# Expert weight pieces laid out as four consecutive rows to a partition, with permuted transposes

## The chip, the core and the metric

The kernel runs on one core of one Trainium2 chip. The metric is the device time of one execution in microseconds (us), as a median over runs. TensorE is PE in the rows, its weight loads are PEld, VectorE is DVE, ScalarE is ACT, GpSimd is POOL, and SyncE, which issues most DMAs here, is SP.

## What is computed

Two sequences of 512 tokens with 1024 features go through a trunk of two layers, all in fp32. Each layer has an attention mixer (latent and window attention in the first, dilated and neighbourhood attention in the second) and then a mixture of 16 experts, in which each expert chooses its 64 best tokens of a sequence:

```
aff = softmax(xt @ w_router);  gate, idx = top_k(aff.T, 64)
xe = xt[idx]
g = xe @ w_gate[e];  u = xe @ w_up[e]              # 1024 x 1024 each
ye = (silu(g) * u) @ w_down[e] * gate
y = zeros.at[idx].add(ye)
```

The two sequences share the weights, so the kernel handles one expert with 128 rows: 64 of the one sequence and 64 of the other.

## The kernel before

The program is a row of stages with a barrier on all engines between them: project, two attention kinds, output (with the router), choose (top 64), experts; then the same for the second layer, and a last norm. The change touches only the two `experts` stages and the helper `load_piece` (L1392), which the stages before them call too, for the first pieces.

An expert has three weight matrices of 1024 x 1024 fp32 (4 MB each). Each is cut by rows into halves of 512 rows, so there are six pieces of 2 MB: gate lo and hi, up lo and hi, down lo and hi. SBUF has a ring with one place for each piece, 16 KB to a partition. A piece is stored as `p c n`: partition p holds four weight rows of 1024 elements, c = 0 to 3. Before the change, slot (p, c) of a piece holds row c * 128 + p of its half.

A product with a piece (`product`, L1475 to 1482) runs c = 0 to 3 and, for each c, two matmuls of 512 columns. The stationary operand is column block `lhs[:, 4 * half + c, :]` of the turned input (128 contraction rows by 128 tokens), the moving operand half a weight row of each partition. The contraction runs over the partitions, so row p of the turned block has to be the feature whose weights lie at (p, c).

The turned inputs are made by `turn` (L1465 to 1470): eight PE transposes of 128x128 in two groups of four, for the gathered rows x of the next expert (into `xT`) and for the hidden rows h of the expert before (into `hT`). A transpose loads 128 columns of the input as stationary operand and streams the 128x128 identity through. ACT copies bank 0 to the first half of the turned tile, DVE bank 1 to the second.

The order of PE in one round e is written by hand: gate lo(e), turn h(e-1), gate hi(e), down lo(e-1), down hi(e-1), up lo(e), turn x(e+1), up hi(e). SP issues the load of a piece as soon as PE has finished with the piece in that place, and the new piece is used one round later. POOL gathers the 128 rows of the next expert from `normed` by an indirect DMA (L1591) and adds the results of the expert before to `residual` by another (L1609). In this trace one fp32 matmul of 512 columns appears as two LDWEIGHTS and two MATMUL records, and one fp32 transpose as one of each.

Of the kernel before, what the change touches and what calls it, by code (L numbers as in the profile page):

```python
# [30 lines left out]
P = 128  # L31
D = 1024
# [19 lines left out]
E = 16  # L52
CAP = 64
F = 1024
# [4 lines left out]
class Steps:  # L59
# [35 lines left out]
    def done(self, name, instruction):  # L95

        step = 1
        while self.names[self.told % self.per] != name:
            assert self.names[self.told % self.per] in self.left_out, name
            self.told += 1  # L100
            step += 1
        self.told += 1
        while self.told % self.per and self.names[self.told % self.per] in self.left_out:
            self.told += 1
            step += 1
        instruction.then_inc(self.sem, step)


def hybrid_trunk(nc, x_in, norm_mix, norm_ffn, norm_final, w_in_ab, q_norm, w_uq, kv_norm, w_ukv, sink,
                 w_out_ab, w_in_cd, rpb_padded, w_out_cd, w_router, w_gate, w_up, w_down,  # L110
                 rope_table, window_table, dilated_table, column_table, y_out):
    with ExitStack() as ctx:
        def sb(name, shape, dt=F32):
            return ctx.enter_context(nc.sbuf_tensor(name, shape, dt))
# [7 lines left out]
        def at(a, offset, pattern):  # L122
            return bass.AP(a.tensor, offset, pattern)
# [8 lines left out]
        ident = sb("ident", [P, P])  # L132
# [7 lines left out]
        bank = [ctx.enter_context(nc.psum_tensor(f"bank{b}", [P, BANK], F32)) for b in range(8)]  # L140
# [955 lines left out]
        def output(inputs):  # L1096
# [47 lines left out]
            def sp(eng):  # L1144
                tile = [[D, P], [1, D]]
                inputs.load_rows(eng, 1)

                load_piece(eng, inputs.layer, 0, 0)
                load_piece(eng, inputs.layer, 0, 1)

                def store_x(t, s):
# [18 lines left out]
                store_x(T - 1, 1)  # L1170
                store_h(T - 1, 1)
                load_piece(eng, inputs.layer, 0, 2)
                load_piece(eng, inputs.layer, 0, 3)
                for s in range(2):
# [217 lines left out]
        def load_piece(eng, layer, e, k):  # L1392
            w, half = SOURCES[k]
            eng.dma_start(ring[:, k * PIECE:(k + 1) * PIECE].rearrange("p (c n) -> p c n", c=4),
                          at(w, (e + layer * E) * (D * F) + half * (D * F // 2), [[F, P], [P * F, 4], [1, F]])
                          ).then_inc(piece_in[k], 16)

        def experts(layer, follow=None):
# [65 lines left out]
                        follow(eng, k)  # L1464

            def turn(eng, src, k, done):
                for c in range(4):
                    mm = eng.transpose(bank[k][:, c * P:(c + 1) * P],  # L1468
                                       src[:, (4 * k + c) * P:(4 * k + c + 1) * P], ident[:, :])
                done(mm)  # L1470

            def pe(eng):
                def body(e, j, left_out):
# [15 lines left out]
                    if "h0" not in left_out:  # L1489
                        for k in range(2):  # L1490
                            eng.wait_ge(dve_s.sem, dve_s.after(f"hidden{k}", e - 1))
                            turn(eng, hidden, k, lambda mm: pe_s.done(f"h{k}", mm))
# [7 lines left out]
                    if "up lo" not in left_out:  # L1500
                        product(4, xT[j], 2, 0, "up lo", e)
                        eng.wait_ge(rows_in[1 - j], e * 8 + (24 if j else 16))
                        for k in range(2):
                            turn(eng, rows[1 - j], k, lambda mm: pe_s.done(f"x{k}", mm))
                        product(4, xT[j], 3, 1, "up hi", e)

                eng.wait_ge(rows_in[0], 16)
                turn(eng, rows[0], 0, lambda mm: mm.then_inc(pe_s.sem, 1))
                turn(eng, rows[0], 1, lambda mm: mm.then_inc(pe_s.sem, 2))
                rounds(eng, pe_s, body)  # L1510
# [292 lines left out]
```

## Time and profile before

| | us |
|---|---|
| median of 3 runs | 2979.7 |
| lowest and highest run | 2979.1, 2984.41 |
| span of the profiled execution | 2978.9 |
| PE busy in the profiled execution | 2808.6 (94%) |
| PE busy in the matmuls of the expert products, L1479 | 1334.7 |
| weight pieces loaded | 192 of 2048 KB |

The profile is of one execution. A row of it sums instructions that have one line and one operation; a stretch (from : to, in us from the start of the span) gives the busy time of each engine in it. The middle of the first expert stage is 742 to 1380 us, and of the second 2260 to 2905 us. "issue" in the rows is waiting that the profile puts down to nothing it shows.

### The profile page before, as it was taken

What the parts mean: (1) busy time and instruction counts of PE and PEld (TensorE: products, weight loads), DVE (VectorE), ACT (ScalarE), POOL (GpSimd) and SP (SyncE); (2) the same over time, 40 slices, a digit from 0 to 9 for tenths busy, and PEclk for the clock granted to TensorE, in tenths of its full rate; (3) what the DMA queues carried; (4) which work ended last, traced back from release to release, by engine and by line L of the source; (5) the groups of instructions that cost most, each with busy time, mean ns of one, the idle gap of its engine ahead of it and who ended that gap; (6) DMA issues with size and microseconds to landing.
All of it is one profiled execution on the core that took longest, in us unless ns stands there. A gap on an engine that the chain in (4) does not pass through costs nothing. (4 is left out here: it accounts for less than half of the span.)

```text
span 2978.9 us, 31400 instructions
## 1 busy us (share of the span) xinstructions
PE 2808.6 (94%) x9840; PEld 1528.3 (51%) x9840; DVE 968.4 (33%) x2002; ACT 497.4 (17%) x1147; POOL 245.4 (8%) x457
## 2 busy tenths in 40 slices
PE   8998999996999999997999989999978999999994
PEld 5665777553444444443444447676543444444442
DVE  2223567224332233222111115554233233323322
ACT  1212446110000000000011014443110000000001
POOL 2221000000000000000000000010000000000002
PEclk9999999997999999998999999999988999999997
DMA  5324243436889988996221132223346998998875
GB/s 182 93 72 115 77 127 102 160 115 254 312 315 323 316 315 315 320 319 238 77 84 45 41 126 57 82 81 128 115 181 228 316 323 311 318 324 314 315 264 190
DMA packets 243226, 594.91 MB, mean 200 GB/s; under 512 B 28640, under 2 KB 101600, under 8 KB 243168
## 3 DMA queue, kind: packets, MB, share of 16 engines
q1 hardware_dynamic: 233664, 559.56, 53.1%
q0 software_dynamic: 9504, 34.61, 4.9%
q8 instruction: 33, 0.54, 0.1%
q14 instruction: 25, 0.20, 0.0%
HBM read 520.72 MB, written 77.07 MB: 201 GB/s over the span
## 5 line engine op out<-in xcount | busy, mean ns | idle before, releaser
L1479 PE MATMUL bank<-ring,arena 128*128 128x512 f32 x3072 | 1334.7, 594 | 3.7 <-issue 1.9
L1479 PEld LDWEIGHTS bank<-ring,arena 128*128 128x128 f32 x3072 | 580.4, 191 | 711.2 <-issue 709.0
L517 PE MATMUL bank<-ring,arena 128*128 128x512 f32 (+3 forms) x1440 | 554.5, 544 | 1.8 <-DVE arena L674 0.9
L517 PEld LDWEIGHTS bank<-ring,arena 128*128 128x128 f32 x1440 | 272.7, 192 | 259.0 <-issue 221.2
L1199 PE MATMUL bank<-ring,arena 128*128 128x512 f32 x512 | 229.7, 603 | 2.2 <-DVE arena L1274 2.2
L1554 DVE RECIPROCAL arena<-arena 128x512 f32<-128x512 f32 x64 | 214.6, 3353 | 2.2
L960 PE MATMUL bank<-arena 128*128 128x512 f32 (+2 forms) x384 | 187.2, 581 | 13.9 <-SPq L187 10.8
L1542 DVE COPY arena<-bank 128x512 f32<-128x512 f32 x66 | 45.6, 691 | 415.8 <-PE bank L1468 415.8
L973 PE MATMUL bank<-arena 128*128 128x64 f32 x1344 | 173.9, 269 | 1.2
L967 PEld LDWEIGHTS bank<-ident,arena 128*128 128x128 f32 x928 | 115.3, 143 | 114.6 <-issue 83.8
L973 PEld LDWEIGHTS bank<-arena 128*128 128x128 f32 x1344 | 165.1, 192 | 6.5 <-DVE arena L1041 4.9
L992 ACT ACTIVATE arena<-arena 128x512 f32<-128x512 f32 (+1 forms) x192 | 127.6, 664 | 190.2 <-DVE arena L1041 111.8
L1514 ACT ACTIVATE arena<-bank 128x512 f32<-128x512 f32 x66 | 39.4, 597 | 701.9 <-PE bank L1468 701.9
L1199 PEld LDWEIGHTS bank<-ring,arena 128*128 128x128 f32 x512 | 96.5, 193 | 113.3 <-issue 113.3
L967 PE MATMUL bank<-ident,arena 128*128 128x128 f32 x928 | 145.8, 276 | 5.0 <-ACT arena L992 3.6
L1021 DVE CUSTOM_DVE_ANT_0 arena<-bank,arena 128x512 f32<-128x512 f32 (+1 forms) x192 | 118.9, 620 | 54.8 <-PE bank L960 39.3
L616 ACT ACTIVATE arena<-bank 128x512 f32<-128x512 f32 (+2 forms) x104 | 57.8, 571 | 468.5 <-PE bank L517 275.1
L1609 POOL DMA_INDIRECT residual<-arena x32 | 51.0, 1594 | 1025.8 <-DVE arena L1560 1025.8
L674 DVE COPY arena<-bank 128x512 f32<-128x512 f32 (+3 forms) x72 | 42.8, 609 | 221.4 <-PE bank L517 155.9
L1031 DVE COPY arena<-bank 128x512 f32<-128x512 f32 (+2 forms) x128 | 82.0, 640 | 91.9 <-PE bank L967 91.1
L1552 DVE TENSOR_SCALAR arena<-arena 128x512 f32<-128x512 f32 x64 | 27.0, 422 | 241.1 <-ACT arena L1524 241.1
L1568 DVE TENSOR_TENSOR arena<-bank,arena 128x512 f32<-128x512 f32 x64 | 41.2, 686 | 196.5 <-PE bank L1479 196.5
(114 smaller groups left out, 1659.8 us busy)
## 6 DMA issues: line engine op xcount, KB each, us to landing
ring<-in_w_gate SPq DMA_DIRECT2D x64, 2048.0 KB, 8.3
ring<-in_w_up SPq DMA_DIRECT2D x64, 2048.0 KB, 9.2
ring<-in_w_down SPq DMA_DIRECT2D x64, 2048.0 KB, 10.3
ring<-in_w_in_cd SPq DMA_DIRECT2D x6, 2048.0 KB, 17.7
arena<-residual SPq DMA_DIRECT2D x24, 512.0 KB, 5.6
arena<-in_x_in SPq DMA_DIRECT2D x16, 512.0 KB, 5.7
mixed<-arena SPq DMA_DIRECT2D x32, 256.0 KB, 2.4
arena<-mixed SPq DMA_DIRECT2D x16, 512.0 KB, 4.2
```

The source lines that it names most:

```text
L517: mm = eng.matmul(bank[bank_of[name]][:, 0:width], lhs(c), rhs_of(c), start=(c == 0), stop=(c == chunks - 1))
L616: act_s.done(name, eng.activation(out, bank[bank_of[name]][0:rows, 0:width], ACT.Copy, **scale))
L960: pe_s.done(f"qk{u}", eng.matmul(bank[u % 4][:, 0:(b1 - b0) * P].rearrange("p (b n) -> p b n", n=P), q[s][:, t, e, :], k[s][:, b0:b1, 0 if ...
L967: mm = eng.transpose(bank[4 + u % 2][:, b * P:(b + 1) * P], p[u % 4][:, b, :], ident[:, :])
L973: mm = eng.matmul(bank[6 + u % 2][:, 0:HD], pT[u % 2][:, b, :], v[s][:, b0 + b, e * HD:(e + 1) * HD], start=(b == 0), stop=(b == b1 - b0 - 1))
L992: act_s.done(f"exp{u}", eng.activation(flat(p[u % 4], n), src, ACT.Exp, bias=stat[:, 0, u:u + 1], scale=-1.0 if biased else 1.0, accum_out ...
L1021: dve_s.done(f"max{u}", eng.tensor_tensor_reduce(flat(masked[u % 4], n), bank[u % 4][:, 0:n], bias, -1.0, BIG, ALU.add, ALU.min, stat[:, 0 ...
L1031: dve_s.done(f"turn{u}", eng.tensor_copy(flat(pT[u % 2], n), bank[4 + u % 2][:, 0:n]))
L1199: mm = eng.matmul(bank[2 + k][:, :], oT[s][:, c, :], wo_ring[:, c, k * BANK:(k + 1) * BANK], start=(c == 0), stop=(c == DC - 1))
L1479: mm = eng.matmul(bank[first_bank + b][:, :], lhs[:, 4 * half + c, :], piece[k][:, c, b * BANK:(b + 1) * BANK], start=(half == 0 and c == ...
L1554: dve_s.done(f"sig{k}", eng.reciprocal(sig[:, half], sig[:, half]))
L1609: eng.indirect_dma_start(out=residual, out_offset=bass.IndirectOffsetOnAxis(ap=index[1 - j], axis=0), in_=y[1 - j], in_offset=None, comput ...
```

## The change

`load_piece` now takes its source with a partition step of four rows: slot (p, c) of a piece holds row 4 * p + c of its half, so the four rows of a partition are one run of 16 KB in HBM, in place of four runs of 4 KB that lie 512 KB apart. The bytes, the places in SBUF, the semaphores and the number of DMAs are the same. To match, the transposes take as stationary operand every fourth column: column p of block (k, c) is feature 512 * k + 4 * p + c, where it was 512 * k + 128 * c + p. In SBUF the 128 elements of one partition that a transpose reads are then 16 bytes apart, where they were 4 bytes apart. The turned tiles keep their shape, and the products, the copies on ACT and DVE and the gathers and scatters are unchanged. `load_piece` is used for all six pieces, and `turn` for x and for h, so both inner dimensions are permuted in the same way as their weights; the output columns of the matrices are not permuted.

```diff
             eng.dma_start(ring[:, k * PIECE:(k + 1) * PIECE].rearrange("p (c n) -> p c n", c=4),
-                          at(w, (e + layer * E) * (D * F) + half * (D * F // 2), [[F, P], [P * F, 4], [1, F]])
+                          at(w, (e + layer * E) * (D * F) + half * (D * F // 2), [[4 * F, P], [F, 4], [1, F]])
                           ).then_inc(piece_in[k], 16)
...
             def turn(eng, src, k, done):
+                columns = src.rearrange("t (h p c) -> t h c p", h=2, c=4)
                 for c in range(4):
-                    mm = eng.transpose(bank[k][:, c * P:(c + 1) * P],
-                                       src[:, (4 * k + c) * P:(4 * k + c + 1) * P], ident[:, :])
+                    mm = eng.transpose(bank[k][:, c * P:(c + 1) * P], columns[:, k, c, :], ident[:, :])
                 done(mm)
```

No instruction moves on any engine. On SP, at the end of the first output stage and the start of the first expert stage, the pieces' DMAs stand where they stood:

```order
-L1394 DMA ring<-in_w_up 128x4x1024 x2
-L1394 DMA ring<-in_w_down 128x4x1024 [waits abo_x_out1,abo_x_out0,stage_ended]
-L1394 DMA ring<-in_w_down 128x4x1024
-L1394 DMA ring<-in_w_gate 128x4x1024 [waits pe_steps,stage_ended]
-L1394 DMA ring<-in_w_gate 128x4x1024 [waits pe_steps]
-L1394 DMA ring<-in_w_up 128x4x1024 [waits pe_steps] x2
+L1394 DMA ring<-in_w_up 128x4096 x2
+L1394 DMA ring<-in_w_down 128x4096 [waits abo_x_out1,abo_x_out0,stage_ended]
+L1394 DMA ring<-in_w_down 128x4096
+L1394 DMA ring<-in_w_gate 128x4096 [waits pe_steps,stage_ended]
+L1394 DMA ring<-in_w_gate 128x4096 [waits pe_steps]
+L1394 DMA ring<-in_w_up 128x4096 [waits pe_steps] x2
```

Only the shape differs: four runs of 1024 elements to a partition have become one of 4096. The waits and their order are the same. On PE the rows are the same but for the line number of the transpose.

## Rows read from the trace of the kernel before

**Rows 1.** Busy time by stretch: first stage start, both expert middles.

```profile
core 0: us, PE busy (x) PEld busy (x) DVE busy (x) ACT busy (x) POOL busy (x), PEclk, DMA share, GB/s
660.00:700.00 40.00, 10.02 (x52) 9.03 (x51) 21.63 (x56) 2.91 (x8) 4.19 (x12) 0.56 0.71 262
...
742.00:1390.00 648.00, 646.14 (x1684) 298.92 (x1683) 184.05 (x165) 44.53 (x75) 45.02 (x73) 1.00 0.89 312
...
2260.00:2905.00 645.00, 645.00 (x1683) 298.76 (x1682) 190.67 (x169) 44.93 (x76) 43.04 (x70) 1.00 0.88 309
```

**Rows 2.** PE in order of time, 959 to 990 us: start, length, line, count.

```profile
959.45 22.48 PE L1479 MATMUL bank<-ring,arena 128*128 128x512 f32 x52
981.76 1.04 PE L1468 MATMUL bank<-ident,arena 128*128 128x128 f32 x8
982.63 7.89 PE L1479 MATMUL bank<-ring,arena 128*128 128x512 f32 x18
```

**Rows 3.** The page's costliest group: busy, mean ns of one, idle before.

```profile
L1479 PE MATMUL bank<-ring,arena 128*128 128x512 f32 x3072 | 1334.7, 594 | 3.7 <-issue 1.9
```

**Rows 4.** What SP and PE waited for, whole span: total us, times, longest.

```profile
SPq L1394 <- PE bank L1479: 1190.1, 178, 20.9
...
PE bank L1468 <- DMA arena<-normed,arena: 12.4, 2, 6.3
```

**Rows 5.** Transposes of the experts by line: ns min/median/max, first and last start.

```profile
L1468 PEld LDWEIGHTS bank<-ident,arena x528: 138/140/230, 698.3 to 2926.8; 128*128 128x128 f32 x176
L1468 PE MATMUL bank<-ident,arena x528: 272/273/448, 698.4 to 2926.9; 128*128 128x128 f32 x176
```

**Rows 6.** Weight loads of other lines: 48 columns, and 128 for a matmul.

```profile
L1222 PEld LDWEIGHTS bank<-ident,arena x8: 103/103/113, 584.3 to 2220.1; 128*48 128x48 f32 x8
L973 PEld LDWEIGHTS bank<-arena x1344: 186/192/192, 422.3 to 2067.2; 128*128 128x128 f32 x192
```

**Rows 7.** Weight loads in a row, in order of time: moving 64 and 16 wide.

```profile
431.19 0.75 PEld L973 LDWEIGHTS bank<-arena 128*128 128x128 f32 x6
659.78 1.75 PEld L1229 LDWEIGHTS bank<-arena 128*128 128x128 f32 x15 [0.24 <-issue]
```

**Rows 8.** SP in order of time, 958 to 1026 us: pieces issued.

```profile
961.49 0.37 SPq L1394 DMA_DIRECT2D ring<-in_w_gate  x1
...
1004.44 0.37 SPq L1394 DMA_DIRECT2D ring<-in_w_gate  x1
```

**Rows 9.** Landing times of a piece (L1394), whole span.

```profile
DMA to landing us min/median/max: 7.7/9.2/17.4
```

**Rows 10.** DMA queues, 742 to 1380 us: packets, MB, share of 16 engines.

```profile
DMA packets 51039, 198.30 MB, mean 311 GB/s; under 512 B 1856, under 2 KB 1856, under 8 KB 51037
...
q1 hardware_dynamic: 46861, 183.06, 78.3%
q0 software_dynamic: 4176, 15.21, 10.1%
```

**Rows 11.** POOL in order of time, 958 to 1050 us: scatter, index, gather.

```profile
976.79 1.59 POOL L1609 DMA_INDIRECT residual<-arena  x1 [31.02 <-DVE arena L1560]
986.11 0.19 POOL L1600 COPY arena<-chosen 128x1 uint32 x1 [7.72 <-DMA residual<-arena]
...
987.50 0.99 POOL L1591 DMA_INDIRECT arena<-normed,arena  x1 [0.81 <-POOL arena L1583]
1019.74 1.60 POOL L1609 DMA_INDIRECT residual<-arena  x1 [31.25 <-DVE arena L1560]
```

**Rows 12.** PE's next turn of x, in order of time.

```profile
1024.71 1.04 PE L1468 MATMUL bank<-ident,arena 128*128 128x128 f32 x8
```

**Rows 13.** Landing times of the gather (L1591), whole span.

```profile
DMA to landing us min/median/max: 4.4/5.5/8.3
```

**Rows 14.** Start of the first expert stage: the last early pieces, the first gather.

```profile
672.93 0.92 SPq L1394 DMA_DIRECT2D ring<-in_w_down  x2
...
693.81 1.22 POOL L1591 DMA_INDIRECT arena<-normed,arena  x1 [0.99 <-POOL arena L1583]
```

## The prediction, made before the changed kernel was run

> **What bounds the kernel now.** I first took the busy time by stretch, to see who is full where the change acts. In the middle of both expert stages PE is busy for 646.14 of 648 us and for all of 645 us, at full granted clock, while the DMA engines are busy for 0.89 and 0.88 of the time [rows 1]. Both are high, so it has to be read which one waits for the other. The list of waits says it: SP, about to load a piece, waited 1190.1 us in total for PE to free the place [rows 4], and PE's only wait for a DMA in these stages is 12.4 us, twice at a stage's start, for the first gathered rows. So the weight stream follows PE, and PE is the bound.
>
> The order of time on PE then gives the price of its two kinds of work. 52 records of a product take 22.48 us; with the length of the last one, 0.59 us [rows 3], taken off, the step is (22.48 - 0.59) / 51 = 0.429 us. Eight transposes take from 981.76 to 982.63, 0.87 us, or 0.109 us each, with no gap on either side [rows 2]. A round of one expert is 96 records of products (48 matmuls of two) and 16 transposes: 96 x 0.429 + 16 x 0.109 = 42.9 us, and two scatters in a row start 42.95 us apart [rows 11]. The round has nothing in it but PE's own stream.
>
> **The load, part one of the change.** It touches 192 pieces of 2 MB. In the middle of the first stage the queue of these loads moved 183.06 MB in 46861 packets, 3.9 KB on the mean [rows 10], that is the runs of 4 KB. Runs of 16 KB can make packets longer and the transfer shorter, but who would use the time? A gate piece is issued at 961.49, when its place is free, and the same place is issued again at 1004.44 [rows 8]. The piece is first needed 16 records (6.9 us) before that, at about 997.5, so 36 us after it was issued; it lands after 9.2 us in the median and 17.4 at most [rows 9]. A faster landing takes time from a slack of 19 us or more, and the load that follows waits for PE all the same. So I cost the load at nothing, from both sides: the gain is nothing since no PE wait ends with a piece, the loss is nothing as long as the stream keeps up. The cover for that is the DMA time that is idle: the two queues use 78.3 + 10.1 = 88.4%, so the loads may use 11.6/78.3 = 15% more engine time [rows 10]. Nothing at the ends is saved either. The first gather starts at 693.81, the last early pieces were issued by 673.85 [rows 14], so even a landing of 17.4 us is over before it.
>
> **The transposes, part two.** This part lies on PE's own stream, so here each nanosecond counts: 528 transposes [rows 5] in 66 bursts of eight. The identity that streams through is read as before. What becomes strided is the stationary operand, the weight load, with 128 elements 16 bytes apart. No row shows a strided load, so I bound it.
>
> Is the load what sets the step of 109 ns? The load's record is 140 ns in a transpose [rows 5], 192 ns in a matmul and 103 ns for 48 columns [rows 6]. A fixed part is hidden in these. In stretches where the moving side is short, loads of the matmul kind stand in a row: (0.75 - 0.19) / 5 = 0.112 us apart with 64 moving columns and (1.75 - 0.19) / 14 = 0.111 us with 16 [rows 7]. So such a load occupies the path for 112 ns and overlaps the matmul before it completely; the step is the longer of load and stream, not their sum. A transpose's load has a record about 50 ns shorter. It thus occupies about 112 - 52 = 60 ns; by columns, (140 - 103) / 80 x 128 = 59 ns. I take half a matmul's load, 56 ns, and keep 60 as the other end. Under a step of 109 ns the load has about 50 ns to spare. The first load of each burst also lies under a matmul step of 429 ns, so at most 7 steps of a burst can grow: 7 x 66 = 462 steps.
>
> The ends are: no effect, 0 us; twice as long, max(109, 112) = 112 ns, 462 x 3 ns = 1.4 us (at 60 ns: 120 - 109 = 11 ns, 5.1 us); four times as long, as if the skipped elements were read too, 224 ns, 462 x 115 ns = 53 us (at 60 ns: 131 ns, 61 us). A gain is excluded, since the identity's stream stays. I take the doubled load, 1.4 us: it is the nearest to rows that exist, the loads of 112 ns [rows 7].
>
> The Trainium skill speaks on this very stride, in the page "SBUF — State Buffer", section "Door 1: The DMA port swizzle": SBUF lines are 16 bytes, an access that goes to a new line pays a penalty, at least two accesses to a line are needed to hide the latency, and yet a step of 4 fp32 is named as free. The change puts each fp32 into a line of its own, just at that step. By the first half of the rule the load grows, as in my first rival; by the second the cost is 0 and the time 2979.7. No row of this trace has such a read, so it can't say which half holds for weight loads.
>
> The results of a transpose are the same in shape, so the copies on ACT and DVE keep their length, and every wait behind them stands under a product of 6.9 us as before.
>
> **The sum.** Profiled span 2978.9 us, plus 0 for the loads, plus 1.4 for the transposes, makes 2980.3. The median of the runs shown is 0.8 us over that execution, which gives **2981.1 us**. A measurement of this kernel can tell some 0.2% (6 us) from no change, so this is "the same".
>
> **Rivals.**
>
> 1. *The strided weight load becomes the bound of the transposes* (slower). It decides from the point where a load takes more than 109 ns, some 1.9 times its length now. At three times, 168 ns, it costs 462 x 59 ns = 27 us, 3007 us; at four times 53 us, **3033 us**. For it: each read uses 4 of 16 consecutive bytes, and PE has no slack at all to hide it [rows 1]. Against it: the load uses only about half of the step. I split it: 15% that it lies between (2986 to 3025 us), 19% that it is about fourfold (3027 to 3042 us).
>
> 2. *The weight stream becomes slower than PE.* Runs of 16 KB change which parts of HBM the 16 DMA engines read side by side, and no row shows such a pattern. From 15% on more engine time the stream would be the bound. At 25% more, the loads take 42.9 x 0.783 x 1.25 = 42.0 us a round and the indirect DMAs 42.9 x 0.101 = 4.3, so 46.3 in place of 42.9: 3.4 x 32 = 109 us, 3090 us. Nothing speaks for it but that it isn't shown; longer runs rather cost less. 4%.
>
> 3. *The indirect DMAs come late.* If packets of 16 KB go ahead of each packet of a gather or scatter, these take longer. Their chain is: scatter at 976.79, over by 986.11, gather at 987.50 [rows 11], landed 5.5 us later [rows 13], its rows turned at 1024.71 at the earliest [rows 12]. It has 31.7 us to spare, twice what scatter and gather take now together, so they would have to become three times as long. I give it no more than 1% of the chance, within the 4% of rival 2.
>
> 4. *The packets don't become longer*, if a run is cut into 4 KB again. Then the load part does nothing at all, and the time is that of the transposes alone; it can't be told from the forecast by time, only by the number of packets.
>
> 5. *Faster.* The only PE wait with a DMA at its end is that of 6.3 us at each stage's start [rows 4]; a less loaded HBM may shorten it a little, and for more than 6 us it would have to vanish in half. I give 4% to this and to anything that I don't see: 2967 to 2973 us.
>
> **How the numbers follow.** Forecast, including rival 4: 58%, 2977 to 2986 us. Rival 1: 15% between and 19% at about 3033 us. Rivals 2 and 3: 4%. Faster: 4%. The forecast and the part between hold 73%, so the range must take in the fourfold load: 2976 to 3038 us; of the likeliest case alone it is 2977 to 2986 us. Within 0.2%: 58% and a small part of the case between, 60%. Slower: 13 + 19 + 4 = 36%. Faster: 4%.
>
> **What would show it.** In the profile of the changed kernel: the landing of a piece and its packets (128 packets of 16 KB to a piece, or 512 of 4 KB) show part one; SP's wait for PE stays near 1190 us or grows. The eight transposes of a burst take 0.87 to 0.90 us from start to next product if I am right, and 1.7 us in the fourfold case; the load's record grows from 140 ns by what the stride adds, and shows that even where the step hides it. Two scatters stay 42.95 us apart, against 44.6 us in the fourfold case. A PE wait that ends with a DMA of `ring` would prove rival 2, one with a gather in the middle of a stage rival 3.

## The result, and the profile after

| | before | changed |
|---|---|---|
| median, 9 runs each | 2980.81 us | 2988.38 us |
| lowest to highest | 2979.10 to 2984.41 | 2986.93 to 2991.72 |
| profiled span | 2978.9 | 2985.7 |
| ratio, with its 95% interval | | 1.0024 (1.0014 to 1.0033) |

The change makes the kernel slower by a quarter of a percent, 7.1 us by the ratio. It lies inside the range (2976 to 3038 us) but above what I held likeliest (2981.1 us; 2977 to 2986 us), and just over the 0.2% within which I had put "no change".

Long runs did come about. The page's section 2 and the landing times of a piece in the changed kernel:

```profile
DMA packets 169498, 594.91 MB, mean 199 GB/s; under 512 B 28640, under 2 KB 101600, under 8 KB 144864
...
DMA to landing us min/median/max: 7.3/8.6/16.5
```

The page before had 243226 packets. The 73728 that are gone are 384 for each of the 192 pieces: 128 packets of 16 KB in place of 512 of 4 KB. A piece lands after 8.6 us where it took 9.2 [rows 9]. The stretches that answer to [rows 1] show who gained by that:

```profile
core 0: us, PE busy (x) PEld busy (x) DVE busy (x) ACT busy (x) POOL busy (x), PEclk, DMA share, GB/s
742.00:1390.00 648.00, 646.14 (x1676) 301.95 (x1675) 184.11 (x165) 44.56 (x75) 45.10 (x73) 1.00 0.86 311
2260.00:2905.00 645.00, 645.00 (x1678) 301.75 (x1677) 185.93 (x166) 44.96 (x76) 43.15 (x70) 1.00 0.85 309
```

Nobody did. DMA's share fell from 0.89 and 0.88 to 0.86 and 0.85, PE is as full as before, and in the same 648 us it got through 1676 matmul records in place of 1684. SP's wait for PE grew from 1190.1 us [rows 4] to 1201.9:

```profile
SPq L1394 <- PE bank L1479: 1201.9, 178, 21.1
```

Most of the loss is in the transposes. First the order of time on PE, as in [rows 2], then the records of the transposes (L1469 is L1468 of before), as in [rows 5]:

```profile
981.53 1.11 PE L1469 MATMUL bank<-ident,arena 128*128 128x128 f32 x8
982.48 7.89 PE L1479 MATMUL bank<-ring,arena 128*128 128x512 f32 x18
```

```profile
L1469 PEld LDWEIGHTS bank<-ident,arena x528: 195/211/231, 697.0 to 2931.8; 128*128 128x128 f32 x176
L1469 PE MATMUL bank<-ident,arena x528: 272/284/461, 697.0 to 2931.9; 128*128 128x128 f32 x176
```

A burst of eight now takes 982.48 - 981.53 = 0.95 us to the next product, where it took 0.87. Over all 66 bursts the medians are 0.953 and 0.873 us, and 66 x 0.080 makes 5.3 us. The weight load's record went from 140 to 211 ns. Not all steps of a burst grew. These are the loads of one burst, first before and then changed:

```profile
981.33 0.14 PEld L1468 LDWEIGHTS bank<-ident,arena 128*128 128x128 f32 x1 [0.24 <-issue]
981.76 0.80 PEld L1468 LDWEIGHTS bank<-ident,arena 128*128 128x128 f32 x7 [0.28 <-issue]
```

```profile
981.10 0.20 PEld L1469 LDWEIGHTS bank<-ident,arena 128*128 128x128 f32 x1 [0.24 <-issue]
981.53 0.92 PEld L1469 LDWEIGHTS bank<-ident,arena 128*128 128x128 f32 x7 [0.23 <-issue]
```

The first load stands alone, under the last matmul of the product, and the other seven follow with the transposes. From the start of one transpose to the next, the medians over all bursts are 109 ns for the first step, as before, then 117, 122 and five times 121 ns. So seven steps grew, by 11.4 ns on the mean.

The rest of the span's 6.8 us shows at the very ends of the expert stages, where PE makes two short pauses before its last 32 records. In the changed kernel, first and second stage:

```profile
1378.47 1.26 PE L1469 MATMUL bank<-ident,arena 128*128 128x128 f32 x8 [0.96 <-DVE arena L1568]
1380.62 15.54 PE L1479 MATMUL bank<-ring,arena 128*128 128x512 f32 x32 [0.90 <-ACT arena L1514]
```

```profile
2930.93 1.26 PE L1469 MATMUL bank<-ident,arena 128*128 128x128 f32 x8 [0.96 <-DVE arena L1568]
2933.08 15.67 PE L1479 MATMUL bank<-ring,arena 128*128 128x512 f32 x32 [0.90 <-ACT arena L1514]
```

In the kernel before, the second of these places reads:

```profile
2925.99 1.16 PE L1468 MATMUL bank<-ident,arena 128*128 128x128 f32 x8 [0.96 <-DVE arena L1568]
2928.05 13.97 PE L1479 MATMUL bank<-ring,arena 128*128 128x512 f32 x32 [0.90 <-ACT arena L1514]
```

The same 32 records, with the same pauses ahead, take 15.54 and 15.67 us, not 13.97. It is the clock. Stretches of the changed kernel there (length, PE busy, PEclk, DMA share, GB/s):

```profile
2933.00:2936.00 3.00, 2.92 (x4) 0.58 0.00 0
2936.00:2939.00 3.00, 3.00 (x7) 0.86 0.00 0
```

The granted clock of 0.58 and 0.86 means that PE ran at 1.2 GHz for a part of these stretches and at 2.4 in the rest; before, it stood at 1.00 throughout. That is 1.6 + 1.7 = 3.3 us. Together with the 5.3 us it is more than the 6.8 us by which the spans differ; the stretches outside the experts came out 1.8 us shorter in this execution (the first turn starts at 697.00 in place of 698.36, and the way from the first expert stage to the second takes 0.4 us less).

### The profile page after: what moved, and what is told of

Same layout as the page of the kernel before. It is cut to its first block and busy times, and to the rows that moved or that the text cites. A ratio compares the mean times of both kernels' runs of the same rounds, so it can differ in the third digit from the quotient of the medians.

```text
span 2985.7 us, 31400 instructions
## 1 busy us (share of the span) xinstructions
PE 2815.2 (94%) x9840; PEld 1537.4 (51%) x9840; DVE 968.9 (32%) x2002; ACT 497.7 (17%) x1147; POOL 245.9 (8%) x457
```

## The experiments

My theory was that the strided weight load costs 5.3 us by itself and the long runs cost and give nothing. The rival was that part of the loss comes with the loads.

**One part alone: the long runs.**

```diff
-                          at(w, (e + layer * E) * (D * F) + half * (D * F // 2), [[F, P], [P * F, 4], [1, F]])
+                          at(w, (e + layer * E) * (D * F) + half * (D * F // 2), [[4 * F, P], [F, 4], [1, F]])
```

> Loads in runs of 16 KB, transposes of consecutive columns as before; the rows of the weights no longer match the columns, so the products are of mismatched rows. Theory (the whole loss lies in the strided weight load of the transposes): a burst of eight transposes takes 0.87 us as before, pieces take 128 packets and land in about 8.6 us, and the time is that of before, within 1 us. Rival (a part of the loss comes with the long runs, by their traffic beside PE or by the clock at the end of the expert stages): 1.5 to 3.5 us slower than before.

Measured: 2982.33 us beside 2981.05 for the kernel before, ratio 1.0002 (0.9993 to 1.0011). The load's record is 140 ns, and the burst takes 984.61 - 983.74 = 0.87 us:

```profile
983.74 1.04 PE L1468 MATMUL bank<-ident,arena 128*128 128x128 f32 x8
984.61 13.90 PE L1479 MATMUL bank<-ring,arena 128*128 128x512 f32 x32
```

Pieces landed in 8.6 us. Both stages ended with 13.97 us for the last 32 records. The long runs alone change nothing that can be told from the noise. The interval of the ratio reaches up to 3.3 us, so by the time alone a small loss isn't excluded; the records show none, neither in the bursts nor at the stage ends.

**The other part alone: the strided transposes**, with loads of 4 KB runs (the change to `turn` only).

> Loads in runs of 4 KB as before, transposes of every fourth column; rows and columns do not match here either. Theory: bursts of 0.95 us, the record of a transpose's load at 211 ns, and 5 to 7 us slower than before, the same as the changed kernel. If the last 32 product records of a stage take 15.6 us in place of 14.0 here too, the clock drop comes from the changed bursts and not from the loads. Rival (part of the loss is the long runs'): at most 5 us slower, and the stage ends as before.

Measured: 2988.01 us, ratio 1.0021 (1.0012 to 1.0030), about the whole loss of the change. Bursts take 0.95 us and the load's record is 211 ns. The first stage ended in 13.97 us, the second in 15.67:

```profile
2932.52 1.25 PE L1469 MATMUL bank<-ident,arena 128*128 128x128 f32 x8 [0.96 <-DVE arena L1568]
2934.68 15.67 PE L1479 MATMUL bank<-ring,arena 128*128 128x512 f32 x32 [0.90 <-ACT arena L1514]
```

So the loss comes with the strided transposes. The clock drop can come without the long runs, and it doesn't come each time.

**Another spacing: two rows together, columns 8 bytes apart.**

```diff
-            eng.dma_start(ring[:, k * PIECE:(k + 1) * PIECE].rearrange("p (c n) -> p c n", c=4),
-                          at(w, (e + layer * E) * (D * F) + half * (D * F // 2), [[4 * F, P], [F, 4], [1, F]])
+            eng.dma_start(ring[:, k * PIECE:(k + 1) * PIECE].rearrange("p (j c n) -> p j c n", j=2, c=2),
+                          at(w, (e + layer * E) * (D * F) + half * (D * F // 2), [[2 * F, P], [2 * P * F, 2], [F, 2], [1, F]])
...
-                columns = src.rearrange("t (h p c) -> t h c p", h=2, c=4)
+                columns = src.rearrange("t (h j p c) -> t h j c p", h=2, j=2, c=2)
...
-                    mm = eng.transpose(bank[k][:, c * P:(c + 1) * P], columns[:, k, c, :], ident[:, :])
+                    mm = eng.transpose(bank[k][:, c * P:(c + 1) * P], columns[:, k, c // 2, c % 2, :], ident[:, :])
```

> Two consecutive rows to a partition twice (runs of 8 KB), transposes of every second column, 8 bytes apart, matched. If the cost depends on how many 16-byte pieces are read, two columns share one, and the load stays hidden under the step of 109 ns: bursts of 0.87 us, the load's record between 140 and 175 ns, time as before within 1 us. Rival (any stride above one costs the same): record 211 ns, bursts 0.95 us, 5 us slower than before.

Measured: 2986.55 us, ratio 1.0018 (1.0009 to 1.0027). The records:

```profile
L1469 PEld LDWEIGHTS bank<-ident,arena x528: 194/209/231, 699.9 to 2935.2; 128*128 128x128 f32 x176
```

That is the rival's case: two columns in one 16-byte piece help next to nothing, the load takes 209 ns and a burst 0.94 us (the median of 66).

**A third spacing: every eighth column, 32 bytes apart.** The rows of a piece are 8 * p + 4 * half + c, so runs stay at 16 KB. A group of four transposes now reads from both halves of the hidden rows, so PE waits for both before the first group.

```diff
-                          at(w, (e + layer * E) * (D * F) + half * (D * F // 2), [[4 * F, P], [F, 4], [1, F]])
+                          at(w, (e + layer * E) * (D * F) + half * (4 * F), [[8 * F, P], [F, 4], [1, F]])
...
-                columns = src.rearrange("t (h p c) -> t h c p", h=2, c=4)
+                columns = src.rearrange("t (p c) -> t c p", c=8)
...
-                    mm = eng.transpose(bank[k][:, c * P:(c + 1) * P], columns[:, k, c, :], ident[:, :])
+                    mm = eng.transpose(bank[k][:, c * P:(c + 1) * P], columns[:, 4 * k + c, :], ident[:, :])
...
+                        eng.wait_ge(dve_s.sem, dve_s.after("hidden1", e - 1))
                         for k in range(2):
-                            eng.wait_ge(dve_s.sem, dve_s.after(f"hidden{k}", e - 1))
```

> Row 8 * p + 4 * half + c, runs of 16 KB at a pitch of 32 KB, transposes of every eighth column, 32 bytes apart, matched; the h turns wait for both halves of the hidden rows. If the load pays per 16-byte piece and every column already has one of its own at stride 4, nothing grows: record 211 ns, bursts 0.95 us, time as the changed kernel within 1.5 us. Rival (the cost grows with the distance): record of 320 ns or more, bursts over 1.5 us, 40 us slower or more.

Measured: 2981.15 us, ratio 1.0001 (0.9992 to 1.0010): as fast as the kernel before, and neither theory had that. Its records and a burst:

```profile
L1469 PEld LDWEIGHTS bank<-ident,arena x528: 185/188/226, 697.4 to 2926.9; 128*128 128x128 f32 x176
```

```profile
980.95 1.04 PE L1469 MATMUL bank<-ident,arena 128*128 128x128 f32 x8
981.83 13.90 PE L1479 MATMUL bank<-ring,arena 128*128 128x512 f32 x32
```

The load is longer than the 140 ns of neighbouring columns but shorter than the 211 ns of every fourth, and a burst takes 0.88 us. By the medians it is 8 ns longer than before (0.881 us), the last steps at 111 to 112 ns in place of 109, which makes 0.5 us in all. So the load's record grew by 48 ns and the steps hardly at all, as the prediction had it: a longer load costs nothing until it is longer than the identity's stream.

**Two odd spacings**, with the same loads and the transposes at `src[:, 4 * k + c : 4 * k + c + s * P]`, each s-th element, s = 3 and 7.

> As the kernel with columns eight apart (runs of 16 KB at 32 KB pitch), but the transposes read every third element, so they don't match the weights: only the spacing in SBUF is tried. Columns 2 and 4 apart cost a load record of 209 and 211 ns and bursts of 0.95 us, columns 8 apart 188 ns and bursts of 0.87 us. Theory A (any spacing but 1 takes twice the stream, and two or more reads in the same 32 bytes cost more on top): 12 bytes apart has nearly three reads in 32 bytes, so about 205 ns and 0.94 us. Theory B (the extra is of powers of two that meet a second reader at the same place): between 188 and 200 ns and bursts of 0.87 to 0.90 us.

> The same with every seventh element, 28 bytes apart: 1.14 reads in 32 bytes. Theory A: about 191 ns and bursts of 0.87 to 0.88 us, near the case of eight. Theory B gives the same or less. A record over 205 ns would speak against both and for a cost that the start address or the order of the reads sets.

Here too rows and columns do not match, and PE waits as with every eighth column. Measured: 2985.24 us for s = 3 and 2989.42 us for s = 7, one run each, beside 2982.52 for the kernel before. Single runs can't be compared closely, so the records have to decide:

```profile
L1468 PEld LDWEIGHTS bank<-ident,arena x528: 188/196/226, 699.6 to 2931.1; 128*128 128x128 f32 x176
```

```profile
L1468 PEld LDWEIGHTS bank<-ident,arena x528: 196/216/230, 696.5 to 2932.2; 128*128 128x128 f32 x176
```

The first is s = 3, with bursts of 0.90 us, the second s = 7, with bursts of 0.97 us. Theory A (reads in the same 32 bytes cost more) wanted about 205 and 191 ns, and theory B wanted both below 200; both fall with the 216 ns of s = 7. All spacings together:

| elements apart | load's record, median ns | burst of eight, median of 66, us |
|---|---|---|
| 1 | 140 | 0.873 |
| 2 | 209 | 0.944 |
| 3 | 196 | 0.904 |
| 4 | 211 | 0.953 |
| 7 | 216 | 0.969 |
| 8 | 188 | 0.881 |

Any spacing over 1 adds 48 to 76 ns to a load, not in the order of the distance. From about 190 ns on, the burst grows with it. What decides between 188 and 216 ns stays open.

**Twice as many transposes**, in the kernel before and in the changed one.

```diff
-                for c in range(4):
+                for c in (0, 1, 2, 3, 0, 1, 2, 3):
```

> The kernel before with each group of four transposes of the experts done twice (the second overwrites the first with the same values): 528 more transposes of consecutive columns. At a step of 109 ns: 57.5 us slower than before, some 3038 us.

> The changed kernel with the same doubling. If the stride costs 10 ns on every transpose and nothing else matters, 528 more steps of 119 ns make it 63 us slower than the changed kernel, some 3051 us, and it lies 10.5 us over the doubled kernel before, plus up to 3.4 us where the clock drops at a stage's end. If the loss of the changed kernel were something else than the bursts, the difference of the two doubled kernels would stay at 7 us.

Measured: 3036.84 us, ratio 1.0190 (1.0176 to 1.0204), and 3050.65 us, ratio 1.0235 (1.0221 to 1.0249), beside 2980.64 for the kernel before. The first lies 56.2 us over it (57.5 expected), and the second 13.8 us over the first (10.5, and up to 3.4 for the clock). The loss grows with the number of strided transposes, from 7.7 us (below, in the same runs) to 13.8. In the two profiles a burst of sixteen takes 965.93 - 964.18 = 1.75 us and 965.62 - 963.69 = 1.93 us. The medians over 66 bursts are 1.747 and 1.923 us, so 66 bursts give 11.6 us of the 13.8; the other 2.2 us are not placed:

```profile
964.18 1.91 PE L1468 MATMUL bank<-ident,arena 128*128 128x128 f32 x16
965.93 27.63 PE L1479 MATMUL bank<-ring,arena 128*128 128x512 f32 x64
```

```profile
963.69 2.09 PE L1469 MATMUL bank<-ident,arena 128*128 128x128 f32 x16
965.62 27.63 PE L1479 MATMUL bank<-ring,arena 128*128 128x512 f32 x64
```

**Both kernels once more, for the clock at the stage ends.**

> The kernel before, unchanged, for a second profile: the last 32 product records of each expert stage. If the clock drop there belongs to the longer bursts, both ends take 13.97 us again; if it is chance of where the pauses fall, one of them may take 15.5 to 17 us.

> The changed kernel, unchanged, for a second profile beside it: bursts of 0.95 us, time some 7 us over before. If the drop belongs to the longer bursts, both stage ends take 15.5 us or more again; if it is chance, at least one may take 13.97 us.

Measured: 2980.65 us (ratio 1.0000, 0.9991 to 1.0009) and 2988.36 us (1.0028, 1.0017 to 1.0039). The kernel before took 13.97 us at both ends again. The changed kernel took 13.97 at the first and 15.67 at the second. Over all profiles with a single set of transposes and whole products, the kernels with bursts of 0.94 us or more had the drop at 6 of 10 stage ends (2 of 2 in the first profile of the changed kernel, 1 of 2 in each of the four others), those with bursts of 0.87 to 0.90 us at none of 10. In five of the six the 32 records took 15.54 or 15.67 us. In the sixth, s = 7, they took 17.02, and there the first pause was 1.56 us and not 0.96, because of the wait for both halves; with the same 1.56 us, the spacings 3 and 8 had no drop. The two doubled kernels had none at four ends. That is not enough to call the longer burst its cause; where the drop comes, it costs 1.6 us or more. At 6 of 10, two ends and 1.7 us it makes some 2 us a run on the average. That is an estimate from few profiles. With it, 5.3 + 2.0 = 7.3 us is close to the 7.1 to 7.7 us of the medians and ratios.

**What longer runs are worth where the stream is the bound.** Both kernels, with half of the matmuls of each product left out:

```diff
-                        for c in range(4):
+                        for c in (0, 3):
```

> The kernel before with runs of 4 KB, and each product with only half of its matmuls (c = 0 and 3 of four): the same bytes are loaded, half of the expert arithmetic is left out. PE needs some 22 us a round and the loads can't keep up with it, so the weight stream becomes the bound. From 88.4% busy DMA queues in a round of 42.9 us the stream needs about 38 us a round: about 4.9 us less in each of 32 rounds, some 2825 us. PE waits for pieces in most rounds.

> The changed kernel (runs of 16 KB, every fourth column) with the same half of the matmuls left out. Theory (longer runs do move faster, and this is hidden in the changed kernel because PE is the bound): the queue share of the loads fell from 78.3% to 75.5%, about 3.5%, so the stream needs about 1.2 us less a round and the time is some 40 us below the same kernel with runs of 4 KB. Rival (the stream is limited by the bytes and not by the runs): the two are within 5 us of each other.

Measured: 2659.99 us with runs of 4 KB (ratio to the kernel before 0.8921, 0.8906 to 0.8936) and 2617.93 us with runs of 16 KB (0.8781, 0.8766 to 0.8795). The second is 42 us faster, although it has the strided transposes. It was expected 40 us below. PE's waits now end with pieces; those of the kernel with 4 KB:

```profile
PE bank L1479 <- DMA ring<-in_w_gate: 99.9, 33, 3.8
PE bank L1479 <- DMA ring<-in_w_down: 75.0, 56, 1.9
PE bank L1479 <- DMA ring<-in_w_up: 55.7, 54, 2.7
```

The same stretch of both, first with 4 KB and then with 16 KB:

```profile
800.00:1100.00 300.00, 225.24 (x554) 97.96 (x555) 106.05 (x97) 25.43 (x43) 26.10 (x44) 0.93 1.03 396
```

```profile
800.00:1100.00 300.00, 229.81 (x579) 103.00 (x580) 110.47 (x99) 26.70 (x45) 27.87 (x47) 0.95 1.01 412
```

Full queues move 396 GB/s with runs of 4 KB and 412 with 16 KB, 4% more, the gathers and scatters included. The long runs also have a price here. A gather lands after 7.5 us in the median with 4 KB and after 10.7 us with 16 KB, a scatter after 9.3 and 12.7 us. With 16 KB, PE waits for a gather once more in each expert stage, after the wait at its start, which it doesn't with 4 KB:

```profile
764.08 1.80 PE L1469 MATMUL bank<-ident,arena 128*128 128x128 f32 x8 [4.85 <-DMA arena<-normed,arena]
2135.65 1.98 PE L1469 MATMUL bank<-ident,arena 128*128 128x128 f32 x8 [4.98 <-DMA arena<-normed,arena]
```

The 42 us are what is left after that. The level was off, though: I expected 2825 us for the short runs and 2660 came out. I had taken the busy share of the queues in the full kernel, 88.4% at 311 GB/s, as work that has to be done. It isn't a measure of that. The stream that was 89% busy at 312 GB/s while it waited for PE moved 396 GB/s when it was kept full.

## Why the prediction was right or wrong

The range holds the result, and its width has a part in that: it was made wide for a fourfold load, which didn't come. The forecast itself, "the same" within 2977 to 2986 us, missed by 2.4 us. The time fell in the part between (2986 to 3025 us), to which I had given 15%.

- **PE is the bound and the weight stream follows it: right.** Long runs alone changed nothing that can be told from the noise (ratio 1.0002), and no middle of a stage has a PE wait with a piece at its end.
- **The load part at 0 us: right.** The margin was far larger than my 15%: the DMA engines could move 396 GB/s with the old runs where 312 were asked for, 27% more. The step that failed here is the reading of the busy share as needed time; it did no harm to the sum, but it mispriced rival 2, which needed a stream 27% slower and not 15%.
- **The step is the longer of load and stream: right**, shown by the load of 188 ns at eight elements apart, with steps of 109 to 112 ns.
- **The strided load at 1.4 us: mis-sized.** I took 56 ns for the load's own time and its double, 112 ns. The other end that I had kept, 60 ns doubled, gives 120 ns and the 5.1 us beside it; the steps that grew settle at 121 ns. That seven steps of a burst can grow, and not the first, was right: 462 steps by 11.4 ns make the 5.3 us. The choice "nearest to rows that exist" was no argument: both ends came from rows, and the load by columns was the one measured on transposes.
- **Nothing on top: wrong.** The sum had no term for the clock. The changed profile has 3.3 us at the two stage ends, and the average over runs is about 2 us by the count above. Rows of before showed the place, two pauses of 0.96 and 0.90 us, but none showed a drop.
- **Rival 1** was the right mechanism, in the lowest part of what I gave it (2986 to 3025 us). The fourfold case, to which I gave 19%, didn't come at any spacing. **Rivals 2, 3 and 5** didn't occur: the gather landed in 5.4 us in the middle of the first stage, its chain kept its slack, and the PE waits at the stages' starts stayed at 12.4 us in all. What rival 3 feared is real where the queues are full: with half of the matmuls left out, the gather landed 3.2 us later behind runs of 16 KB, and PE waited for it. **Rival 4** is out by the packets.
- **The rule of the Trainium skill** ("SBUF — State Buffer", section "Door 1: The DMA port swizzle"): that a step of 4 fp32 is free does not hold for this weight load, 211 ns against 140. That two accesses to a line hide the latency doesn't either: at a step of two elements there are two, and the load took 209 ns. That going to a new line costs fits the 211 ns, but it doesn't explain the 188 ns at eight apart, where each access goes to a new line as well.

## What to carry to other kernels

Longer runs are worth something only where the weight stream is waited for: here 42 us with half of the arithmetic left out, and nothing in the real kernel. Whether it is waited for stands in the waits, not in the busy share of the DMA engines, which was 0.89 with a quarter more to give. Where the queues are full, longer runs also make small transfers beside them land later. An access pattern that a layout forces on a bound engine has to be priced there; if rows must be permuted for the loads, try another spacing, since every eighth column cost some 0.5 us in the records where every fourth cost 5.3 us, but no permuted version beat the plain one.

## What the runs showed of the hardware

- The time of a weight load of 128 fp32 columns depends on their spacing and not by distance: 140, 209, 196, 211, 216 and 188 ns at 1, 2, 3, 4, 7 and 8 elements.
- A load's record can grow by 48 ns with a step between transposes of 109 to 112 ns, where it was 109, and by 71 ns with one of 121 ns.
- A DMA with one run to a partition was issued by SP in 333 ns, and one with four runs in 373 ns (medians of 64).
- Full queues of 2 MB loads, with gathers and scatters beside them, moved 396 GB/s in packets of 4 KB and 412 GB/s in packets of 16 KB. A gather landed after 7.5 us beside the first and 10.7 us beside the second.
- After the same two pauses of 0.96 and 0.90 us the granted clock fell in some executions and not in others; the 32 records after them took 13.97, 15.54 or 15.67 us. After pauses of 1.56 and 0.90 us they took 13.97 us, and once 17.02.
